# Storing the two halves of a weight unit as interleaved pairs in a two-block transformer on one core

## The chip, the cores and the metric

The kernel runs on one core of a Trainium2 chip, in one launch. The metric is the device time in microseconds from the first to the last instruction of a run; three runs of the kernel before gave 1748.44 us as their median (1747.19 to 1749.85).

## What is computed

A 256-token sequence of width 1024 goes through two layers of a first block and one layer of a second, all in float32. Cut to what matters here:

```python
for i in range(2):                                        # first block
    x = x + 0.5 * swiglu(rms_norm(x, ln_ffn1[i]), ffn1_w_gu[i], ffn1_w_down[i])   # width 2816
    h = rms_norm(x, ln_mix[i])
    x = x + (even_mixer if i == 0 else odd_mixer)(h, ...)  # latent attention + delta rule / sparse attention
    x = x + 0.5 * swiglu(rms_norm(x, ln_ffn2[i]), ffn2_w_gu[i], ffn2_w_down[i])
    x = x + sigmoid(rms_norm(x, ln_ple[i]) @ ple_w_gate[i]) * (p[i] @ ple_w_in[i])
h = rms_norm(x, norm1_g)                                  # second block
pa, pb, pg, pc = split(h @ w_in)                          # gated conv, linear recurrence, gates, rwkv
m = gate_a * y_a + gate_b * y_b + gate_c * y_c
x = x + m @ w_out
x = x + square(relu(rms_norm(x, norm2_g) @ mlp_w1)) @ mlp_w2   # width 4096
return rms_norm(x, final_g)
```

Nearly all arithmetic is in the weight products `h @ w`.

## The kernel before, in words

All weights are cut into 514 *units* of 128 partitions x 1024 float32 numbers. They come from memory in the order of use, into a ring of three slots, `raw`. A product in float32 accuracy is made out of single-pass products of rounded numbers: ScalarE copies a unit from `raw` into `w_hi` with rounding to the type fp32r (`act_split`, the activation on L456), VectorE subtracts that from `raw` and writes the remainder into `w_lo` (`dve_split`, the tensor_tensor on L464), and TensorE then multiplies low by high, high by low and high by high into one PSUM bank (`mm3`, L477; all matmuls are issued in `mm`, on L475). The activations are held in the same way as a rounded half and a remainder (`h`, `h_of_feed_forward`, `a_hi` and `a_lo`).

`w_hi` and `w_lo` are two tensors of three slots each, so that the 1024 numbers of one half lie side by side. In most products the weights are the *stationary* operand: a LDWEIGHTS reads 128 columns of one half (512 bytes of a partition, side by side), and a MATMUL then streams 256 or 512 token columns, the *moving* operand, past them. In a few products the parts are swapped, and 256 or 512 columns of a weight unit are the moving operand: the mlp's down products (`tokens_down`, L820), the value projection of the first mixer (L1390) and of the second (L2039).

The stages, in order: `ffn0`, `even`, `ffn1`, `ple0`, `ffn2`, `odd`, `ffn3`, `ple1`, `second`, `mlp`. In a gated feed-forward each of 22 rounds takes three units: two up products (`up_product`, L496: for each of 8 row tiles, w_lo against 256 columns, and w_hi against 512, which are the rounded half and the remainder of h side by side), and one down product (`down`, L837: 8 x 3 matmuls of 256 columns). A projection of the other stages (`linear`, L507) is 8 x 3 matmuls of 256 columns. `opening` and `early_units` do the same in another order at the start of a stage.

What sets the order: each engine runs its own program, written out by hand. `s_hi` and `s_lo` count split units, `s_prod` counts units whose products are done. ScalarE splits unit u when its load has landed and the products of unit u-3 are done; VectorE follows on `s_hi`; TensorE waits for `s_lo`; SyncE (SP) loads unit u+3 into `raw` once `s_lo` says that unit u has been split. The rest of ScalarE's and VectorE's work stands between the splits in their queues. POOL issues only a few transfers. Small spare tensors (`in_front_of_h`, `behind_h`, `in_front_of_a`) fix at which addresses h, raw, the weights and a begin; the edit leaves them as they are.

Of the kernel before, what the change touches and what calls it, by code (L numbers as in the profile page):

```python
# [11 lines left out]
T, P, D = 256, 128, 1024  # L12
KT = D // P
NB = T // P
UNIT = 8 * P
RING = 3
TURN = 6
D_FF, D_FF2 = 2816, 4096
FJ, FJ2 = D_FF // P, D_FF2 // P
# [267 lines left out]
def build(nc, a_x, a_p, a_w, a_par, a_con, a_gain, out, stages=STAGES):  # L287
    f32 = mybir.dt.float32
    ALU, ACT, AX = mybir.AluOpType, mybir.ActivationFunctionType, mybir.AxisListType
    MUL, ADD, SUB, MAXOP, MINOP = ALU.mult, ALU.add, ALU.subtract, ALU.max, ALU.min  # L290
    par_off, par_n = offsets(PARAMS)
    con_off, con_n = offsets(CONSTS)
    unit_base, total_units = {}, 0
# [5 lines left out]
    with ctx:  # L299
# [6 lines left out]
        def sbr(name, shape):  # L306

            return ctx.enter_context(nc.sbuf_tensor(name, shape, mybir.dt.float32r))
# [6 lines left out]
        h_hi, h_lo = h[:, :, 0, :], h[:, :, 1, :]  # L315
        sb("behind_h", [P, 88])
        raw = sb("raw", [P, RING, UNIT])
        w_hi, w_lo = sbr("w_hi", [P, RING, UNIT]), sbr("w_lo", [P, RING, UNIT])
        sb("in_front_of_a", [P, 8])
        a_hi, a_lo = sbr("a_hi", [P, 3, T]), sbr("a_lo", [P, 3, T])  # L320
        par = sb("par", [P, par_n + 8])[:, 0:par_n]
# [5 lines left out]
        ps = ctx.enter_context(nc.psum_tensor("ps", [P, 8, 512], f32))  # L327
# [6 lines left out]
        def f(ap):  # L334

            return ap.bitcast(f32)
# [44 lines left out]
        s_hi, s_lo, s_prod = sem("hi_ready"), sem("lo_ready"), sem("products_done")  # L381
# [41 lines left out]
        V, A, TE = nc.vector, nc.scalar, nc.tensor  # L423
        
        class Links:


            n = 0
# [15 lines left out]
        narrow = {unit_base["second"] + 2 + 12 * t + 7: 5 * P for t in range(KT)} if "second" in stages else {}  # L444
        if "even" in stages:
            narrow[unit_base["even"] + 25] = 2 * P
        split_next = {"act": 0, "dve": 0}

        def act_split(act, last, i=None):

            for u in range(split_next["act"], min(last + 1, total_units)):
                act.wait_ge(arrived[u % RING], loads(u, i))
                if u >= RING:
                    act.wait_ge(s_prod, nth(u - RING, i))
                n = narrow.get(u, UNIT)
                A.activation(w_hi[:, u % RING, 0:n], raw[:, u % RING, 0:n], ACT.Copy).then_inc(s_hi, 1)  # L456
                split_next["act"] = u + 1

        def dve_split(dve, last, i=None):

            for u in range(split_next["dve"], min(last + 1, total_units)):
                dve.wait_ge(s_hi, nth(u, i))
                n = narrow.get(u, UNIT)
                V.tensor_tensor(w_lo[:, u % RING, 0:n], raw[:, u % RING, 0:n], f(w_hi[:, u % RING, 0:n]), SUB)\  # L464
                    .then_inc(s_lo, 1)
                split_next["dve"] = u + 1

# [6 lines left out]
        def mm(o, lhsT, rhs, start=True, stop=True):  # L474
            return TE.matmul(o, lhsT, rhs, start=start, stop=stop, skip_group_check=True)  # L475

        def mm3(o, l_hi, l_lo, r_hi, r_lo, start=True, stop=True):  # L477

            mm(o, l_lo, r_hi, start, False)
            mm(o, l_hi, r_lo, False, False)  # L480
            return mm(o, l_hi, r_hi, False, stop)

        def wmm(o, u, k, hi, lo, start=True, stop=True):

            c_ = slice(k * P, k * P + P)
            return mm3(o, w_hi[:, u % RING, c_], w_lo[:, u % RING, c_], hi, lo, start, stop)

        def after_mixer(n):

# [6 lines left out]
        def up_product(pe, u, bank, n, i=None):  # L496

            h_ = h_of(n)

            pe.wait_ge(s_lo, nth(u, i))  # L500
            for k in range(KT):
                c_ = slice(k * P, k * P + P)
                mm(ps[:, bank, 0:T], w_lo[:, u % RING, c_], h_[:, k, 0, :], k == 0, False)
                last = mm(ps[:, bank, :], w_hi[:, u % RING, c_], h_[:, k, :, :].rearrange("p a t -> p (a t)"), False, k == KT - 1)
            last.then_inc(s_prod, 1)

        def linear(pe, u, o, i=None, norm=None, normed=None, src=None):  # L507
# [12 lines left out]
        def early_units(pe, n, tiles):  # L520

            src = h_of(n)
            for i_, (u, bank) in enumerate(tiles):
                pe.wait_ge(s_lo, nth(u))
                for k in range(KT):
                    c_ = slice(k * P, k * P + P)
                    if i_ == 0 and k % 2 == 0:
                        pe.wait_ge(s_hr, h_at[n] + k // 2 + 1)
                    mm(ps[:, bank, 0:T], w_lo[:, u % RING, c_], src[:, k, 0, :], k == 0, False)
                    mm(ps[:, bank, 0:T], w_hi[:, u % RING, c_], src[:, k, 0, :], False, False)  # L530
            for i_, (u, bank) in enumerate(tiles):
                for k in range(KT):
                    if i_ == 0 and k % 2 == 0:
                        pe.wait_ge(s_h, h_at[n] + k // 2 + 1)
                    last = mm(ps[:, bank, 0:T], w_hi[:, u % RING, k * P:k * P + P], src[:, k, 1, :], False, k == KT - 1)
                last.then_inc(s_prod, 1)


# [73 lines left out]
        def opening(pe, n, tiles):  # L612

            h_ = h_of(n)

            last_pair = KT - 2 if n and stages[n - 1] in n_ple else KT
            for ks in (range(last_pair), range(last_pair, KT)):
                for i_, (u, bank) in enumerate(tiles):
                    pe.wait_ge(s_lo, nth(u))
                    o = ps[:, bank, 0:T]  # L620
                    for k in ks:
                        c_ = slice(k * P, k * P + P)
                        if i_ == 0 and k % 2 == 0:
                            pe.wait_ge(s_hr, h_at[n] + k // 2 + 1)
                        mm(o, w_lo[:, u % RING, c_], h_[:, k, 0, :], k == 0, False)
                        mm(o, w_hi[:, u % RING, c_], h_[:, k, 0, :], False, False)
            for i_, (u, bank) in enumerate(tiles):
                o = ps[:, bank, T:2 * T]
                for k in range(KT):
                    if i_ == 0 and k % 2 == 0:  # L630
                        pe.wait_ge(s_h, h_at[n] + k // 2 + 1)
                    last = mm(o, w_hi[:, u % RING, k * P:k * P + P], h_[:, k, 1, :], False, k == KT - 1)
                last.then_inc(s_prod, 1)

        def sum_bank(n):
# [177 lines left out]
        def ffn_pe(pe, f_):  # L813
# [6 lines left out]
            def tokens_down(u, j, q, stop):  # L820

                b_, c_ = slice(q // 2 * P, q // 2 * P + P), slice(q % 2 * 512, q % 2 * 512 + 512)
                l_hi, l_lo = a_hi[:, j % f_.bufs, b_], a_lo[:, j % f_.bufs, b_]
                return mm3(ps[:, q, :], l_hi, l_lo, w_hi[:, u % RING, c_], w_lo[:, u % RING, c_], False, stop)

            def last_tokens_down():

# [220 lines left out]
        def even_mixer():  # L1048
            u0 = unit_base["even"]
# [92 lines left out]
            def pe_prog(pe):  # L1142
# [65 lines left out]
                for n in range(22):  # L1208
# [5 lines left out]
                    elif n > 1:  # L1214
                        linear(pe, u0 + n, ps[:, in_bank(n), 0:T], normed=order["even"] if n == 5 else None,
                               src=h_two if n < 5 else None)
# [169 lines left out]
                pe.wait_ge(s_lo, nth(u0 + 26))  # L1386
                for tb in range(NB):
                    for k in range(2):
                        sl, c_ = (u0 + 26) % RING, slice(k * 512, (k + 1) * 512)
                        last = mm3(ps[:, (5, 4)[tb], :], h_hi[:, 3 + k, blk(tb)], h_lo[:, 3 + k, blk(tb)],  # L1390
                                   w_hi[:, sl, c_], w_lo[:, sl, c_], k == 0, k == 1)
                last.then_inc(s_prod, 1)
                Yl(3)
                sa("qn1")
# [3 lines left out]
                for tb in range(NB):  # L1398
                    for j in range(2):
                        o = 8 * tb + 4 * j  # L1400
                        mm(ps[:, 7, o:o + 4], sq_r[:, j, blk(tb)], C("quads"), True, False)
                        for m in (2 * j, 2 * j + 1):
                            last = mm(ps[:, 7, 8 * tb + 2 * m:8 * tb + 2 * m + 2], sq_n[:, m, blk(tb)],
                                      pairs[:, 0:P:64], False, m % 2 == 1)
# [7 lines left out]
                for j in range(2):  # L1412
                    last = mm(ps[:, 6, j * T:j * T + T], heads_r[0:16, j, :], rrk[0:16, :])
# [12 lines left out]
                for g in range(4):  # L1426
                    last = mm(ps[:, 0, g * P:g * P + P], TTf[:, 0, g, :], vtok[:, 0, g, :])
# [4 lines left out]
                for g in range(4):  # L1432
                    last = mm(ps[:, 2, g * P:g * P + P], ktok[:, g, :], vn[:, g, :])
                did(last, "st0")
                for g in range(4):
                    last = mm(ps[:, 1, g * P:g * P + P], vn[:, g, :], QK[:, 0, g, :])
# [4 lines left out]
                for g in range(4):  # L1441
                    last = mm(ps[:, 0, g * P:g * P + P], kbg[:, g, blk(1)], St[:, g, :])
# [433 lines left out]
        def odd_mixer():  # L1876
            u0 = unit_base["odd"]
# [43 lines left out]
            def pe_prog(pe):  # L1921
# [108 lines left out]
                for n in (15, 16):  # L2030
                    if n == 15:
                        sa("in13")
                    u = u0 + n
                    pe.wait_ge(s_lo, nth(u))
                    for j in range(4):
                        k = 4 * (n - 15) + j
                        for tb in range(NB):
                            c_ = slice(j * T, j * T + T)
                            last = mm3(ps[:, 4 + tb, 0:T], h_hi[:, k, blk(tb)], h_lo[:, k, blk(tb)],  # L2039
                                       w_hi[:, u % RING, c_], w_lo[:, u % RING, c_], k == 0, k == 7)  # L2040
                    last.then_inc(s_prod, 1)
                    between(n)
                sa("sdq")
# [1422 lines left out]
```

## Time and profile before

| | |
|---|---|
| median of the three runs shown | 1748.44 us (1747.19 to 1749.85) |
| span of the profiled execution | 1751.1 us; the page gives it no other time |
| TensorE matmul / weight load busy | 97% / 90% |
| VectorE / ScalarE busy | 74% / 57% |
| chain that ended last | PE 83%, VectorE 8%, ScalarE 6% |
| mean granted TensorE clock | 0.982 of full speed |

A matmul row's duration is longer than the distance to the next matmul's start, since matmuls are pipelined; how fast a stream goes is read from the distances between starts. PEld rows are the weight loads, which run while an earlier matmul streams. A row that says x7 has seven instructions merged, from the first one's start to the last one's end. The line named for a wait or an operation is a line of the listing above; L475 holds every matmul that the weight products issue.

### The profile page before, as it was taken

The numbers are of one execution on the slowest core, as the hardware profiler recorded it, in microseconds if no ns is written. First come the engines' busy times: TensorE is split into PE (matmuls) and PEld (weight loads), VectorE is DVE, ScalarE is ACT, GpSimd is POOL, SyncE is SP. The second block draws the span as 40 slices with busy tenths as digits, with TensorE's granted clock in tenths as the row PEclk, the third lists the DMA queues.
The fourth block names the chain that finished last, engine by engine and source line by source line (L and its number), as shares of the span: only waits on it lengthen the run. The fifth ranks groups of instructions, "written<-read, shape, count | busy, mean of one in ns | idle before, by whom it ended". The sixth has DMA issues, their size and how long they took to land.

```text
span 1751.1 us, 37772 instructions
## 1 busy us (share of the span) xinstructions
PE 1694.5 (97%) x14502; PEld 1574.0 (90%) x14502; DVE 1290.8 (74%) x2137; ACT 995.2 (57%) x1562; POOL 3.0 (0%) x9
## 2 busy tenths in 40 slices
PE   7999999999999999999999999989999999899998
PEld 6999899889999989999988999989999998798887
DVE  6777867658777887777767777877788774567776
ACT  5544655445444664445555554668877875444444
POOL 0000000000000000000000000000000000000000
PEclk9999989899999999999999999999999999999999
DMA  6555533115555445554425655545555550055554
GB/s 230 191 188 183 165 133 109 62 31 181 192 191 188 162 166 192 180 191 157 145 82 173 192 188 188 169 157 184 178 183 191 175 163 4 23 174 179 186 187 144
DMA packets 75864, 278.24 MB, mean 159 GB/s; under 512 B 8432, under 2 KB 8688, under 8 KB 75248
## 3 DMA queue, kind: packets, MB, share of 16 engines
q1 hardware_dynamic: 75168, 273.58, 47.9%
q0 software_dynamic: 592, 3.15, 0.5%
q8 instruction: 81, 1.33, 0.3%
q14 instruction: 23, 0.19, 0.0%
HBM read 274.59 MB, written 2.10 MB: 158 GB/s over the span
## 4 chain that ended last, share of the span: by engine, by line
PE 83%; DVE 8%; ACT 6%; issue 2%; DMA 0%; DVEq 0%; SPq 0%; ACTq 0%
PE ps L475 82%; DVE w_lo L464 2%; ACT w_hi L456 2%; PE ps L2471 1%; DVE rstd L607 1%; DVE x L943 1%; DVE h L568 1%; DVE arena L911 0%; DVE arena L915 0%; ACT L2796 0%; ACT L2780 0%; DMA x<-x_t 0%; DVE arena L656 0%; DVE a_lo L931 0%; ACT arena L2133 0%
## 5 line engine op out<-in xcount | busy, mean ns | idle before, releaser
L475 PE MATMUL ps<-h,w_hi 128*128 128x256 f32 (+1 forms) x3380 | 732.4, 307 | 0.0
L464 DVE TENSOR_TENSOR w_lo<-raw,w_hi 128x1024 fp32r<-128x1024 f32 x514 | 621.4, 1215 | 86.6 <-ACT w_hi L456 67.5
L456 ACT ACTIVATE w_hi<-raw 128x1024 fp32r<-128x1024 f32 x514 | 538.6, 1050 | 223.2 <-PE ps L475 205.6
L475 PE MATMUL ps<-h,w_lo 128*128 128x256 f32 x2026 | 583.9, 289 | 22.9 <-DVE w_lo L464 15.6
L475 PEld LDWEIGHTS ps<-h,w_hi 128*128 128x128 f32 x3380 | 554.4, 193 | 26.4
L475 PEld LDWEIGHTS ps<-h,w_lo 128*128 128x128 f32 x2026 | 390.5, 193 | 30.1 <-DVE w_lo L464 14.5
L475 PE MATMUL ps<-h_of_feed_forward,w_hi 128*128 128x512 f32 (+1 forms) x1088 | 351.5, 374 | 0.0
L475 PE MATMUL ps<-h_of_feed_forward,w_lo 128*128 128x256 f32 x1000 | 278.8, 281 | 0.8 <-issue 0.6
L896 ACT ACTIVATE arena<-ps 128x256 f32<-128x256 f32 x208 | 79.1, 382 | 267.7 <-PE ps L475 267.7
L475 PEld LDWEIGHTS ps<-h_of_feed_forward,w_hi 128*128 128x128 f32 x1088 | 198.3, 188 | 36.3
L475 PE MATMUL ps<-a_hi,w_lo 128*128 128x256 f32 x776 | 218.3, 281 | 4.2 <-DVE a_lo L931 4.2
L475 PE MATMUL ps<-a_lo,w_hi 128*128 128x256 f32 x776 | 217.3, 280 | 0.0
L475 PE MATMUL ps<-a_hi,w_hi 128*128 128x256 f32 x776 | 217.0, 280 | 0.0
L911 DVE TENSOR_TENSOR arena<-ps,arena 128x256 f32<-128x256 f32 x208 | 88.3, 424 | 142.3 <-ACT arena L896 141.8
L475 PEld LDWEIGHTS ps<-h_of_feed_forward,w_lo 128*128 128x128 f32 x1000 | 188.2, 188 | 3.3 <-ACT h_of_feed_forward L560 1.2
L475 PEld LDWEIGHTS ps<-a_hi,w_lo 128*128 128x128 f32 x776 | 146.0, 188 | 6.0 <-DVE a_lo L931 5.5
L475 PEld LDWEIGHTS ps<-a_lo,w_hi 128*128 128x128 f32 x776 | 146.1, 188 | 3.2
L475 PEld LDWEIGHTS ps<-a_hi,w_hi 128*128 128x128 f32 x776 | 146.0, 188 | 0.0
L475 PE MATMUL ps<-arena 64*64 64x64 f32 (+6 forms) x2808 | 112.5, 241 | 9.3 <-issue 6.7
L475 PEld LDWEIGHTS ps<-arena 64*64 64x64 f32 (+3 forms) x2808 | 100.0, 147 | 21.3 <-issue 12.5
L915 DVE TENSOR_TENSOR arena<-arena,rstd 128x256 f32<-128x256 f32 x176 | 75.1, 427 | 6.0
L901 ACT ACTIVATE arena<-arena 128x256 f32<-128x256 f32 x120 | 50.1, 418 | 46.2 <-DVE arena L917 33.3
(354 smaller groups left out, 1447.9 us busy)
## 6 DMA issues: line engine op xcount, KB each, us to landing
raw<-weights SPq DMA_DIRECT2D x514, 512.0 KB, 3.4
con<-shape_constants SPq DMA_DIRECT2D x1, 1618.0 KB, 10.5
x<-x_t SPq DMA_DIRECT2D x1, 1024.0 KB, 5.0
stored<-x POOLq DMA_DIRECT2D x1, 1024.0 KB, 4.8
x<-stored POOLq DMA_DIRECT2D x1, 1024.0 KB, 7.9
out_t<-arena SPq DMA_DIRECT2D x4, 256.0 KB, 2.1
arena<-p_t POOLq DMA_DIRECT2D x2, 256.0 KB, 4.1
arena<-final_gain POOLq DMA_DIRECT2D x1, 512.0 KB, 4.6
```

What stands on the lines that cost most here:

```text
L456: A.activation(w_hi[:, u % RING, 0:n], raw[:, u % RING, 0:n], ACT.Copy).then_inc(s_hi, 1)
L464: V.tensor_tensor(w_lo[:, u % RING, 0:n], raw[:, u % RING, 0:n], f(w_hi[:, u % RING, 0:n]), SUB)\
L475: return TE.matmul(o, lhsT, rhs, start=start, stop=stop, skip_group_check=True)
L568: last = V.scalar_tensor_tensor(h_[:, k, 1, :], x[:, k, :], G(NORM_OF[stages[n]], k), f(h_[:, k, 0, :]), MUL, SUB)
L607: V.reciprocal(rstd[:, :], rstd[:, :]).then_inc(s_vc, vc.step())
L896: A.activation(rest[:, half, j % f_.bufs, :], ps[:, f_.bank(j) + half, T:2 * T], ACT.Copy).then_inc(s_rest, 1)
L901: A.activation(sg[:, j % f_.bufs, :], tg[:, j % f_.bufs, :], ACT.Silu if f_.gated else ACT.Square).then_inc(s_nl, 1)
L911: V.tensor_tensor((t_, u_)[half], ps[:, f_.bank(j) + half, 0:T], rest[:, half, j % f_.bufs, :], ADD)\
L915: V.tensor_tensor((t_, u_)[half], (t_, u_)[half], rstd[:, :], MUL).then_inc((s_scl, s_fac)[half], 1)
L943: V.scalar_tensor_tensor(x[:, pair_of(b), :], ps[:, b, :].rearrange("p (a t) -> p a t", a=2), 0.5, x[:, pair_of(b), :], MUL, ADD).then_inc ...
L2471: last = TE.transpose(ps[:, bk, s * P:s * P + P], two_heads(src, c, s), ident)
```

## The change

`w_hi` and `w_lo` become one tensor `w` of three slots of 2048 numbers. In a slot, element n of the unit has its rounded half at place 2n and its remainder at 2n+1. ScalarE writes the halves at a step of 8 bytes, VectorE reads them and writes the remainders at that step, and every LDWEIGHTS of a weight half reads 128 numbers at that step, over 1024 bytes instead of 512. Units in the set `planar`, those that are the moving operand, keep the old form inside a slot: 1024 halves, then 1024 remainders. They are 1 unit of `even`, 2 of `odd` and the 32 down units of `mlp`, 35 of 514. No instruction is added, removed or moved, and the size in memory is the same.

```diff
-        w_hi, w_lo = sbr("w_hi", [P, RING, UNIT]), sbr("w_lo", [P, RING, UNIT])
+        w_ = sbr("w", [P, RING, 2 * UNIT])
...
+        planar = set()
+        if "even" in stages:
+            planar.add(unit_base["even"] + 26)
+        if "odd" in stages:
+            planar |= {unit_base["odd"] + 15, unit_base["odd"] + 16}
+        if "mlp" in stages:
+            planar |= set(range(unit_base["mlp"] + 2, unit_base["mlp"] + 2 * FJ2 - 4, 2))
+            planar |= {unit_base["mlp"] + 2 * FJ2 - n for n in (3, 2, 1)}
+
+        def parts_of(u, cols):
+
+            slot = w_[:, u % RING, :]
+            if u in planar:
+                return slot[:, 0:UNIT][:, cols], slot[:, UNIT:2 * UNIT][:, cols]
+            pairs_ = slot.rearrange("p (n two) -> p n two", two=2)
+            return pairs_[:, cols, 0], pairs_[:, cols, 1]
...
-                A.activation(w_hi[:, u % RING, 0:n], raw[:, u % RING, 0:n], ACT.Copy).then_inc(s_hi, 1)
+                A.activation(parts_of(u, slice(0, n))[0], raw[:, u % RING, 0:n], ACT.Copy).then_inc(s_hi, 1)
...
-                V.tensor_tensor(w_lo[:, u % RING, 0:n], raw[:, u % RING, 0:n], f(w_hi[:, u % RING, 0:n]), SUB)\
+                hi, lo = parts_of(u, slice(0, n))
+                V.tensor_tensor(lo, raw[:, u % RING, 0:n], f(hi), SUB)\
                     .then_inc(s_lo, 1)
...
-            return mm3(o, w_hi[:, u % RING, c_], w_lo[:, u % RING, c_], hi, lo, start, stop)
+            return mm3(o, *parts_of(u, c_), hi, lo, start, stop)
...
-                mm(ps[:, bank, 0:T], w_lo[:, u % RING, c_], h_[:, k, 0, :], k == 0, False)
-                last = mm(ps[:, bank, :], w_hi[:, u % RING, c_], h_[:, k, :, :].rearrange("p a t -> p (a t)"), False, k == KT - 1)
+                mm(ps[:, bank, 0:T], parts_of(u, c_)[1], h_[:, k, 0, :], k == 0, False)
+                last = mm(ps[:, bank, :], parts_of(u, c_)[0], h_[:, k, :, :].rearrange("p a t -> p (a t)"), False, k == KT - 1)
...
-                return mm3(ps[:, q, :], l_hi, l_lo, w_hi[:, u % RING, c_], w_lo[:, u % RING, c_], False, stop)
+                return mm3(ps[:, q, :], l_hi, l_lo, *parts_of(u, c_), False, stop)
```

The other matmuls of weight units (`early_units`, `opening`, the two value projections) change in the same way.

## Rows read from the trace of the kernel before

**Rows 1.** The page: busy time by engine, and the chain that ended last.
```profile
PE 1694.5 (97%) x14502; PEld 1574.0 (90%) x14502; DVE 1290.8 (74%) x2137; ACT 995.2 (57%) x1562; POOL 3.0 (0%) x9
...
PE 83%; DVE 8%; ACT 6%; issue 2%; DMA 0%; DVEq 0%; SPq 0%; ACTq 0%
```

**Rows 2.** Windows: a feed-forward, a stretch of second, mlp; columns as headed.
```profile
core 0: us, PE busy (x) PEld busy (x) DVE busy (x) ACT busy (x) POOL busy (x), PEclk, DMA share, GB/s
27.00:195.00 168.00, 167.86 (x1126) 154.62 (x1127) 130.53 (x205) 83.81 (x123) 0.00 (x0) 1.00 0.58 187
1220.00:1240.00 20.00, 20.00 (x167) 19.75 (x167) 16.24 (x32) 18.27 (x32) 0.00 (x0) 1.00 0.49 167
1572.00:1736.00 164.00, 164.00 (x825) 138.25 (x824) 114.14 (x175) 81.25 (x117) 0.00 (x0) 1.00 0.56 179
```

**Rows 3.** Timeline, PE, first feed-forward: start us, length us, line, operands.
```profile
109.87 0.39 PE L475 MATMUL ps<-h,w_hi 128*128 128x512 f32 x1
110.10 0.28 PE L475 MATMUL ps<-h,w_lo 128*128 128x256 f32 x1
...
110.56 0.39 PE L475 MATMUL ps<-h,w_hi 128*128 128x512 f32 x1
110.79 0.28 PE L475 MATMUL ps<-a_hi,w_lo 128*128 128x256 f32 x1
...
112.89 0.28 PE L475 MATMUL ps<-a_hi,w_lo 128*128 128x256 f32 x1
```

**Rows 4.** Timeline, PE, a projection of second.
```profile
1370.74 0.28 PE L475 MATMUL ps<-h,w_lo 128*128 128x256 f32 x1
1370.86 0.40 PE L475 MATMUL ps<-h,w_hi 128*128 128x256 f32 x2
...
1373.23 0.28 PE L475 MATMUL ps<-h,w_lo 128*128 128x256 f32 x1
```

**Rows 5.** Timeline, PE, a projection of ple0.
```profile
611.92 0.28 PE L475 MATMUL ps<-h,w_lo 128*128 128x256 f32 x1
612.04 0.40 PE L475 MATMUL ps<-h,w_hi 128*128 128x256 f32 x2
...
612.64 0.28 PE L475 MATMUL ps<-h,w_lo 128*128 128x256 f32 x1
```

**Rows 6.** Groups by shape, PE: count | busy us, mean ns | idle us before.
```profile
L475 PE MATMUL ps<-h,w_lo 128*128 128x256 f32 x2026 | 583.9, 289 | 22.9 <-DVE w_lo L464 15.6 <-DVE h L652 4.8 <-ACT h L560 1.9
L475 PE MATMUL ps<-h,w_hi 128*128 128x256 f32 x2708 | 497.3, 286 | 0.0
L475 PE MATMUL ps<-h_of_feed_forward,w_lo 128*128 128x256 f32 x1000 | 278.8, 281 | 0.8 <-issue 0.6
L475 PE MATMUL ps<-h,w_hi 128*128 128x512 f32 x672 | 235.1, 392 | 0.0
L475 PE MATMUL ps<-a_hi,w_lo 128*128 128x256 f32 x776 | 218.3, 281 | 4.2 <-DVE a_lo L931 4.2
L475 PE MATMUL ps<-h_of_feed_forward,w_hi 128*128 128x256 f32 x176 | 31.6, 281 | 0.0
L475 PE MATMUL ps<-con,arena 128*128 128x1 f32 x124 | 15.0, 253 | 1.1 <-DVE arena L602 0.8 <-ACT arena L1543 0.3
```

**Rows 7.** Timeline, PE: matmuls of one moving column, each with its weight load.
```profile
277.10 0.92 PE L475 MATMUL ps<-con,arena 128*128 128x1 f32 x7
```

**Rows 8.** Groups by shape, weight loads of 128 and of 64 columns.
```profile
L475 PEld LDWEIGHTS ps<-h_of_feed_forward,w_hi 128*128 128x128 f32 x1088 | 198.3, 188 | 36.3
L475 PEld LDWEIGHTS ps<-con,arena 128*64 128x64 f32 x64 | 3.3, 135 | 1.5 <-DVE arena L3023 0.6
```

**Rows 9.** Groups by shape: L3156 at a step of 8 bytes, L3210 side by side, the splits.
```profile
L3156 DVE TENSOR_TENSOR x<-x,arena 128x512 f32<-128x512 f32 x2 | 1.4, 694 | 0.1
L3210 DVE TENSOR_TENSOR arena<-arena 128x512 f32<-128x512 f32 x4 | 2.8, 692 | 0.1
L464 DVE TENSOR_TENSOR w_lo<-raw,w_hi 128x1024 fp32r<-128x1024 f32 x505 | 614.4, 1222 | 86.6 <-ACT w_hi L456 67.5
L456 ACT ACTIVATE w_hi<-raw 128x1024 fp32r<-128x1024 f32 x505 | 532.2, 1056 | 214.0 <-PE ps L475 196.4 <-DMA raw<-weights 11.3 <-DVE arena L2949 2.7
L456 ACT ACTIVATE w_hi<-raw 128x640 fp32r<-128x640 f32 x8 | 5.9, 738 | 9.2 <-PE ps L475 9.2
```

More of the change, by code:

```diff
@@ L528, in early_units @@
                         pe.wait_ge(s_hr, h_at[n] + k // 2 + 1)
-                    mm(ps[:, bank, 0:T], w_lo[:, u % RING, c_], src[:, k, 0, :], k == 0, False)
-                    mm(ps[:, bank, 0:T], w_hi[:, u % RING, c_], src[:, k, 0, :], False, False)
+                    mm(ps[:, bank, 0:T], parts_of(u, c_)[1], src[:, k, 0, :], k == 0, False)
+                    mm(ps[:, bank, 0:T], parts_of(u, c_)[0], src[:, k, 0, :], False, False)
             for i_, (u, bank) in enumerate(tiles):
@@ L534, in early_units @@
                         pe.wait_ge(s_h, h_at[n] + k // 2 + 1)
-                    last = mm(ps[:, bank, 0:T], w_hi[:, u % RING, k * P:k * P + P], src[:, k, 1, :], False, k == KT - 1)
+                    last = mm(ps[:, bank, 0:T], parts_of(u, slice(k * P, k * P + P))[0], src[:, k, 1, :], False, k == KT - 1)
                 last.then_inc(s_prod, 1)
@@ L624, in opening @@
                             pe.wait_ge(s_hr, h_at[n] + k // 2 + 1)
-                        mm(o, w_lo[:, u % RING, c_], h_[:, k, 0, :], k == 0, False)
-                        mm(o, w_hi[:, u % RING, c_], h_[:, k, 0, :], False, False)
+                        mm(o, parts_of(u, c_)[1], h_[:, k, 0, :], k == 0, False)
+                        mm(o, parts_of(u, c_)[0], h_[:, k, 0, :], False, False)
             for i_, (u, bank) in enumerate(tiles):
@@ L631, in opening @@
                         pe.wait_ge(s_h, h_at[n] + k // 2 + 1)
-                    last = mm(o, w_hi[:, u % RING, k * P:k * P + P], h_[:, k, 1, :], False, k == KT - 1)
+                    last = mm(o, parts_of(u, slice(k * P, k * P + P))[0], h_[:, k, 1, :], False, k == KT - 1)
                 last.then_inc(s_prod, 1)
@@ L1388, in pe_prog @@
                     for k in range(2):
-                        sl, c_ = (u0 + 26) % RING, slice(k * 512, (k + 1) * 512)
+                        c_ = slice(k * 512, (k + 1) * 512)
                         last = mm3(ps[:, (5, 4)[tb], :], h_hi[:, 3 + k, blk(tb)], h_lo[:, 3 + k, blk(tb)],
-                                   w_hi[:, sl, c_], w_lo[:, sl, c_], k == 0, k == 1)
+                                   *parts_of(u0 + 26, c_), k == 0, k == 1)
                 last.then_inc(s_prod, 1)
@@ L2039, in pe_prog @@
                             last = mm3(ps[:, 4 + tb, 0:T], h_hi[:, k, blk(tb)], h_lo[:, k, blk(tb)],
[L2040 removed]
+                                       *parts_of(u, c_), k == 0, k == 7)
                     last.then_inc(s_prod, 1)
```

## The prediction

> **What bounds the kernel now.** I read the page first: the matmul row is busy for 97% of the span, the weight-load row for 90%, and 83% of the chain that ended last is PE [rows 1]. Busy matmuls prove little, so the windows by stage come next. In a feed-forward, in `second` and in `mlp` PE is covered from end to end at a granted clock of 1.00 (the 2.4 GHz level), while VectorE has 37 us of 168 free and ScalarE 84 [rows 2]. So in these stages the end is set by how close matmuls follow each other, and the timeline gives that. In the feed-forward 18 down matmuls of 256 columns take 112.89 - 110.79 = 2.10 us, 116.7 ns each; two up pairs (256 and 512 columns) take 110.56 - 109.87 = 0.69 us, 345 ns a pair, so that 228 ns are left for the 512 columns [rows 3]. In a projection of `second` 21 matmuls of 256 columns take 1373.23 - 1370.74 = 2.49 us, 118.6 ns each [rows 4]; in one of `ple0` six take 0.72 us, 120.0 ns [rows 5]. The same shape thus runs at three paces, all at full clock.
>
> What stands beside such a matmul is the load of the next 128 weights. Seven matmuls of a single moving column take 0.92 us, of which the last one's own length is 0.253 us, so one follows the other after (0.92 - 0.25) / 6 = 111 ns [rows 6, 7]; with nothing to stream, that is the pace of the load. A load of 128 columns is recorded with 188 ns and one of 64 with 135 [rows 8]: 0.83 ns a column. So matmul and load are nearly tied, 117 to 120 ns against 111. With 512 columns the load ends within the first half, and the second half costs at most 228 - 116.7 = 111 ns: an upper estimate of what 256 columns cost when no load runs beside them. Between 5 and 9 ns of each 256-column matmul are thus more than either stream needs alone.
>
> **The change part by part.** No instruction comes, goes or moves, so no queue is passed and no wait added; three kinds of operand change their step.
>
> *The splits on VectorE.* It reads the halves and writes the remainders at 8 bytes. The trace has such an operation: L3156 reads and writes x at every second number, and 512 elements take 694 ns against 692 side by side [rows 9]. Cost: 0.
>
> *The splits on ScalarE.* It writes at 8 bytes; no row shows that engine doing so. Lower bound 0, since even the form side by side is no faster than 0.83 ns an element ((1056 - 738) / 384 [rows 9]) and a step gives no reason for gain; upper bound one more 0.83 ns an element, 0.85 us a split. I take 0, from the nearest row, VectorE's. In a feed-forward ScalarE's 84 free microseconds would cover 60 splits of +0.85 us (51 us); in `second` it is busy 18.27 of 20 us [rows 2], and the cover is thin (a rival below).
>
> *The planar units.* They keep their order inside a slot; 0.
>
> *The weight loads.* Matmuls of 256 columns on stationary units: 2026 + 2708 + 1000 + 176 and three times 776 (the low-by-high down form and its two companions), 8238 in all [rows 6]. Of these, 2708 x 1.5 = 4062 belong to projections, which run at 118.6; the other 4176 run at about 116.7. After the change a load covers 1024 bytes at 0.83 ns a column, 8 bytes each, and the moving operand covers 1024 bytes in nearly the same time; before, the load went through 512. The two streams therefore advance side by side instead of one overtaking the other. Where they share something in the memory, that either frees them from each other or keeps them in step at the bad place. Outer bound of a gain: all 256-column matmuls down to 111 ns, 4062 x 7.6 + 4176 x 5.7 = 55 us. Outer bound of a loss: a load that takes twice its time per column, 111 + 128 x 0.83 = 217 ns, then sets the pace: 4062 x 98 + 4176 x 100 = +817 us. The first fits a stream that meets no other, the second a load that can fetch only one number where it now fetches two; no row shows a stationary read at a step. VectorE's row speaks against the second. I take the nearest row to the first that is actually sustained in this kernel, 116.7 ns: the projections fall from 118.6 to 116.7, 4062 x 1.9 = 7.7 us, all of it on PE's own path, because PE is covered in those windows. The 512-column matmuls hide the load either way: 0.
>
> Sum: -7.7 us. The span of the profiled execution is 1751.1 us and the median of the runs 1748.4, 0.15% less; the difference carries over, so 1748.4 - 7.7 = 1741 us. Next late would be ScalarE in `second`, at 18.27 of then 19.7 us.
>
> The Trainium skill speaks against this gain: "TensorE: Matmul & The Clock Gate", section "Step-by-step: what each phase is for", says that weights and moving data come through two independent read ports, so that a load takes no bandwidth from a running matmul. By it the sum is 0, and the same-time case below holds. The trace agrees only in part, since one shape runs at 116.7, 118.6 and 120.0 ns at one clock [rows 3 to 5].
>
> **The rivals.**
> *Nothing moves.* The 5 to 9 ns over 111 are the two streams' own handshake, or the moving stream's own fetch, and the load keeps its pace. For it: 512 columns cost 228, close to twice 116.7, so most of the excess goes with moving columns and not with loads. Against: three paces of one shape. 1748 us.
>
> *Slower: the streams collide all along.* A load that touches twice the addresses, in step with the moving operand, meets it more often. All 256-column matmuls then run at the worst pace seen, 120.0 ns [rows 5]: 4062 x 1.4 + 4176 x 3.3 = +19.5 us, 1768 us. It decides as soon as the common pace is above 117.6, the weighted mean of now. For it: the load has only 6 to 9 ns of room. Against: the nearest step-of-8 row cost nothing.
>
> *Slower: ScalarE becomes the bound in `second`.* With 24 x 118.6 ns = 2.85 us a unit, seven units lie in 20 us, so ScalarE has 1.73 / 7 = 0.25 us a unit free. A split longer than 1056 + 250 ns decides; at +0.85 us each of about 98 units costs 0.60 us, +59 us, 1807 us.
>
> *A load twice as long:* up to 1748 + 817 = 2565 us.
>
> *Much faster:* the streams part completely, down to 1748 - 55 = 1693 us. For it only the 111 ns of the second half.
>
> *That the change doesn't do what it says* I exclude: the operands' steps are in the text of the kernel.
>
> **How the numbers follow.** The forecast, 1741 us, gets 0.36; much faster 0.08; nothing moves 0.27; collision 0.17; ScalarE 0.08; the long load 0.04. Below 0.2% (3.5 us, about what a measurement of this kernel can tell from none) counts as same. So faster 0.44, same 0.27, slower 0.29. The range 1715 to 1775 holds the forecast, nothing moves, most of the collision case (0.15) and the near part of much faster (0.03), 0.81 together; the likeliest case's own range is 1735 to 1745, projections at 115.5 to 118 ns.
>
> **What would show it.** In the changed profile: the down matmuls' distance near 116.7 and the projections' falling to it (forecast), staying at 118.6 (nothing moves), or both at 120 and above (collision); LDWEIGHTS still at 188 ns, and single-column matmuls, whose operands don't change, still at 111; L456's successor at 1.05 us and L464's at 1.22. The prediction is wrong if the loads lengthen beyond the matmuls, if ScalarE's split passes 1.3 us, or if the 512-column pairs move from 345 ns, since I gave them nothing.

## The result, and the profile after

The changed kernel takes 1776.05 us (median of four runs, 1772.54 to 1776.7), the kernel before 1747.82 beside it (1747.1 to 1749.85): a ratio of 1.0157, interval 1.0142 to 1.0171. It is slower by 28 us, where 7.7 us less were forecast, and it lies 1 us above the range. The profiled execution has a span of 1774.3 us against 1751.1, a difference of 23.2.

The page of the changed kernel, in its first part and its chain:

```profile
span 1774.3 us, 37772 instructions
...
PE 1717.4 (97%) x14502; PEld 1604.7 (90%) x14502; DVE 1292.8 (73%) x2137; ACT 1033.7 (58%) x1562; POOL 3.0 (0%) x9
...
PE 87%; DVE 7%; ACT 4%; issue 2%; DMA 0%; SPq 0%; DVEq 0%; ACTq 0%
```

Against [rows 1], the matmul row grew by 22.9 us, about as much as the span, and the weight-load row by 30.7; VectorE stayed, ScalarE grew by 38.5, and the chain has more PE and less of both. So the time is on PE's own path. The windows of the changed kernel, a feed-forward and a stretch of `second`, columns as in [rows 2]:

```profile
27.00:195.00 168.00, 168.00 (x1108) 156.31 (x1108) 127.89 (x200) 86.25 (x120) 0.00 (x0) 1.00 0.57 184
1220.00:1240.00 20.00, 20.00 (x168) 19.65 (x167) 16.32 (x28) 15.61 (x22) 0.00 (x0) 1.00 0.53 174
```

The clock is the same 1.00 and PE is covered as before, but 1108 matmuls fit in the feed-forward's 168 us instead of 1126. Nobody waits longer; the matmuls follow each other more slowly. The timeline of the changed kernel's first feed-forward, PE:

```profile
106.15 5.79 PE L492 MATMUL ps<-h,w 128*128 128x256 f32 x32
111.78 0.28 PE L492 MATMUL ps<-a_hi,w 128*128 128x256 f32 x1
111.89 0.28 PE L492 MATMUL ps<-a_lo,w 128*128 128x256 f32 x1
...
114.55 0.28 PE L492 MATMUL ps<-a_hi,w 128*128 128x256 f32 x1
```

The first row holds 16 up pairs (a row that merges instructions carries the shape of the first of them): (111.78 - 106.15) / 16 = 352 ns a pair. The 23 down matmuls behind it take (114.55 - 111.78) / 23 = 120.4 ns each. In `second`, 52 matmuls on h (same view):

```profile
1368.83 6.44 PE L492 MATMUL ps<-h,w 128*128 128x256 f32 x52
```

That is (6.44 - 0.28) / 51 = 120.8 ns. The following means are of the distances between the starts of neighbouring matmuls (for a pair, from one pair's start to the next one's), over the whole of each trace; distances with a pause or a stretch of half clock in them (above 140 ns for 256 columns) are left out:

| | before | after | difference x count |
|---|---|---|---|
| projections on h, 256 columns | 118.07 ns | 120.67 | 4062 x 2.60 = +10.6 us |
| down, 256 columns | 116.90 | 120.66 | 2328 x 3.76 = +8.8 us |
| up pairs, 256 + 512 columns | 346.99 | 351.32 | 1584 x 4.33 = +6.9 us |
| mlp's planar down, 512 columns | 233.4 | 233.4 | 0 |

The sum, some 26 us, is 3 us more than the difference of the spans and lies inside the interval of the ratio (24.8 to 29.9 us). The products whose weight loads step by 8 bytes became slower, the planar ones did not. The groups by shape of the changed kernel (count | busy us, mean ns | idle before):

```profile
L492 PEld LDWEIGHTS ps<-h_of_feed_forward,w 128*128 128x128 f32 x2088 | 321.6, 195 | 35.7 <-ACT h_of_feed_forward L577 1.1 <-issue 0.7
L492 PEld LDWEIGHTS ps<-w,a_hi 128*128 128x128 f32 x256 | 48.1, 188 | 11.5
L481 DVE TENSOR_TENSOR w<-raw,w 128x1024 fp32r<-128x1024 f32 x505 | 616.4, 1223 | 116.6 <-ACT w L472 103.1
L472 ACT ACTIVATE w<-raw 128x1024 fp32r<-128x1024 f32 x505 | 577.7, 1146 | 209.6 <-PE ps L492 192.5 <-DMA raw<-weights 11.0 <-DVE arena L2966 2.7
```

A load at a step is recorded 7 ns longer than the 188 of [rows 8]; one that reads a_hi side by side (second row) is not longer. VectorE's split kept its time [rows 9], ScalarE's grew from 1056 to 1146 ns. Two suspects are left: the reading of the stationary operand at a step, and the writing at a step, which lengthened ScalarE's split.

### The profile page after: what moved, and what is told of

Its sections match the earlier page's. It is cut to its first block, busy times and chain, and to the rows that moved or that the text cites. A ratio compares the mean times of both kernels' runs of the same rounds, so it can differ in the third digit from the quotient of the medians.

```text
span 1774.3 us, 37772 instructions
## 1 busy us (share of the span) xinstructions
PE 1717.4 (97%) x14502; PEld 1604.7 (90%) x14502; DVE 1292.8 (73%) x2137; ACT 1033.7 (58%) x1562; POOL 3.0 (0%) x9
## 4 chain that ended last, share of the span: by engine, by line
PE 87%; DVE 7%; ACT 4%; issue 2%; DMA 0%; SPq 0%; DVEq 0%; ACTq 0%
PE ps L492 86%; DVE w L481 2%; ACT w L472 1%; PE ps L2488 1%; DVE rstd L624 1%; DVE h L585 1%; DVE arena L928 0%; DVE x L960 0%; DMA x<-x_t 0%; DVE arena L673 0%; ACT h L577 0%; DVE arena L932 0%; ACT arena L2150 0%; ACT arena L599 0%; DVE a_lo L948 0%
## 5 line engine op out<-in xcount | busy, mean ns | idle before, releaser
L492 PE MATMUL ps<-h,w 128*128 128x256 f32 (+1 forms) x5406 | 766.9, 303 | 22.7 <-DVE w L481 15.7
L492 PEld LDWEIGHTS ps<-h,w 128*128 128x128 f32 x5406 | 721.8, 200 | 53.2 <-DVE w L481 14.5
L472 ACT ACTIVATE w<-raw 128x1024 fp32r<-128x1024 f32 x514 | 584.6, 1140 | 218.6 <-PE ps L492 201.5
L481 DVE TENSOR_TENSOR w<-raw,w 128x1024 fp32r<-128x1024 f32 x514 | 623.4, 1215 | 116.6 <-ACT w L472 103.1
L492 PE MATMUL ps<-h_of_feed_forward,w 128*128 128x256 f32 (+1 forms) x2088 | 366.5, 331 | 0.7 <-issue 0.6
L492 PEld LDWEIGHTS ps<-h_of_feed_forward,w 128*128 128x128 f32 x2088 | 321.6, 195 | 35.7 <-ACT h_of_feed_forward L577 1.1
L492 PE MATMUL ps<-a_hi,w 128*128 128x256 f32 x1552 | 296.7, 284 | 4.2 <-DVE a_lo L948 4.2
L492 PEld LDWEIGHTS ps<-a_hi,w 128*128 128x128 f32 x1552 | 253.6, 197 | 5.7 <-DVE a_lo L948 5.5
L492 PE MATMUL ps<-a_lo,w 128*128 128x256 f32 x776 | 220.2, 284 | 0.0
L492 PEld LDWEIGHTS ps<-a_lo,w 128*128 128x128 f32 x776 | 152.6, 197 | 3.1
```

What stands on the lines that cost most here:

```text
L472: A.activation(parts_of(u, slice(0, n))[0], raw[:, u % RING, 0:n], ACT.Copy).then_inc(s_hi, 1)
L481: V.tensor_tensor(lo, raw[:, u % RING, 0:n], f(hi), SUB)\
```

## The experiments

**1. Pairs written, but read side by side.** The change alters writing and reading; this undoes the reading, the next the writing.

```diff
-        def parts_of(u, cols):
+        def parts_of(u, cols, read=True):          # both splits call it with False
...
-            if u in planar:
+            if u in planar or read:
```

> The changed kernel, in which ScalarE and VectorE still write and read pairs at a step of 8 bytes, but every weight load reads 128 numbers side by side out of the slot (so the weights multiplied are a mixture of halves and remainders: this part of the computation is changed). Theory A (the stationary read at a step costs the time): loads return to 188 ns, down matmuls follow each other at 116.7 ns and not 120.8, the 512-column ones at 229.5 and not 233, and the time is that of the kernel before, 1748 us, within 4 us; ScalarE's split stays at 1140 ns. Theory B (the writes at a step disturb TensorE's reads): the time stays at 1776 us, matmuls at 120.8. Theory C (ScalarE's longer split, 1140 against 1050 ns, holds the stages back): also 1776 us, with matmuls closer together and gaps between units.

Measured: 1749.51 us, ratio 1.0005 (0.999 to 1.002). Its timeline in the first feed-forward, PE, and its groups by shape:

```profile
104.47 5.71 PE L492 MATMUL ps<-h,w 128*128 128x256 f32 x32
110.02 0.28 PE L492 MATMUL ps<-a_hi,w 128*128 128x256 f32 x1
...
112.70 0.28 PE L492 MATMUL ps<-a_hi,w 128*128 128x256 f32 x1
```
```profile
L492 PEld LDWEIGHTS ps<-a_lo,w 128*128 128x128 f32 x776 | 145.9, 188 | 3.3
...
L472 ACT ACTIVATE w<-raw 128x1024 fp32r<-128x1024 f32 x505 | 574.6, 1140 | 199.1 <-PE ps L492 182.8 <-DMA raw<-weights 10.5 <-DVE arena L2966 2.7
```

A pair is back at (110.02 - 104.47) / 16 = 347 ns, a down matmul at (112.70 - 110.02) / 23 = 116.5, a load at 188, while ScalarE's split is as long as in the changed kernel. The longer split alone costs nothing that shows in the ratio (more on this under 2); the slow matmuls are gone with the stepped reading.

**2. Written side by side, read as pairs.** As above with the condition turned round:

```diff
+            if u in planar or not read:
```

> The changed kernel, in which ScalarE and VectorE write halves and remainders side by side, 1024 numbers each, as before, but every load of a stationary weight half reads 128 numbers at a step of 8 bytes out of the slot (the weights multiplied are thus the wrong ones of the slot: this part of the computation is changed). Theory A (stationary read): 1776 us within 4 us, loads 196 ns, down matmuls 120.8 ns, while ScalarE's split is back at 1050 ns. Theories B and C (the splits' step): 1748 us, matmuls 116.7 ns.

Measured: 1770.89 us, ratio 1.0117 (1.0092 to 1.0141). Its timeline in the first feed-forward, PE, and its split on ScalarE:

```profile
106.71 5.79 PE L492 MATMUL ps<-h,w 128*128 128x256 f32 x32
112.33 0.28 PE L492 MATMUL ps<-a_hi,w 128*128 128x256 f32 x1
...
115.11 0.28 PE L492 MATMUL ps<-a_hi,w 128*128 128x256 f32 x1
```
```profile
L472 ACT ACTIVATE w<-raw 128x1024 fp32r<-128x1024 f32 x505 | 532.3, 1056 | 226.7 <-PE ps L492 208.7 <-DMA raw<-weights 11.3 <-DVE arena L2966 2.8
```

A pair takes (112.33 - 106.71) / 16 = 351 ns and a down matmul (115.11 - 112.33) / 23 = 120.9; over the whole trace the projections run at 120.65. All three are as in the changed kernel, with ScalarE at its old 1056. Reading at a step is the cause of most of the loss: 1.17 of 1.57% by the ratios, 20 of 27 us. The two intervals just miss each other, and the rest is not in the paces of the weight products, which are the same in both traces. Runs at one granted clock can be compared more closely: at 0.985 the changed kernel took 1774.3 us and experiment 2 1770.9 (means of two runs each), and at 0.986 experiment 1 took 1749.3 (five runs) and the kernel before beside it 1747.1 (three). So the stepped writes may cost some 2 to 3.5 us by themselves, which these few runs suggest and don't show.

**3. Loads at several steps, measured by themselves.** Behind the last product of the kernel before stand groups of 32 matmuls whose results nobody reads; the step of the load, the moving columns and the start change from group to group (wf is w_hi and hf is h, each as one row of numbers):

```diff
+        for _ in range(32):                         # one group: 256 columns, a load at 8 bytes
+            TE.matmul(ps[:, 7, 0:256], wf[:, 0:256:2], hf[:, 0:256], start=True, stop=True, ...)
```

> The kernel before, with 37 groups of 32 matmuls behind its last product on TensorE, whose results nobody reads: stationary operand from the weight halves at steps of 0 to 8 numbers, 64, 256 or 512 moving columns, and at steps 1 and 2 eleven different starts of the stationary operand. Theory A1 (the load at a step is slower by itself, and sets the pace at 256 columns): with 64 moving columns, where only the load counts, one matmul follows the other after 111 ns at step 1, about 120 at step 2, more at steps 4 and 8; with 256 columns the larger of that and 117; with 512 columns 230 at every step up to 4. Theory A2 (load and moving stream meet in the memory): with 64 columns 111 ns at steps 1 and 2, with 256 columns 117 and 121, with 512 columns 230 and 233, at step 0 less than at step 1, and at step 2 the distance depends on where the stationary operand starts relative to the moving one, by 3 ns or more from start to start, more so than at step 1.

Its timeline, PE, one row a group; steps in numbers of 4 bytes: 1, 2, 3, 4, 8 with 64 moving columns, then 2, 3, 4, 8, 0 with 256 columns, last one whose moving operand steps by 2:

```profile
1741.29 3.75 PE L3329 MATMUL ps<-h,w_hi 128*128 128x64 f32 x32
1744.86 7.01 PE L3331 MATMUL ps<-h,w_hi 128*128 128x64 f32 x32
1751.68 7.01 PE L3333 MATMUL ps<-h,w_hi 128*128 128x64 f32 x32
1758.51 7.64 PE L3335 MATMUL ps<-h,w_hi 128*128 128x64 f32 x32
1765.96 7.79 PE L3337 MATMUL ps<-h,w_hi 128*128 128x64 f32 x32
...
1779.81 4.03 PE L3341 MATMUL ps<-h,w_hi 128*128 128x256 f32 x32
1783.68 5.72 PE L3343 MATMUL ps<-h,w_hi 128*128 128x256 f32 x32
1789.23 7.63 PE L3345 MATMUL ps<-h,w_hi 128*128 128x256 f32 x32
1796.70 7.84 PE L3347 MATMUL ps<-h,w_hi 128*128 128x256 f32 x32
1804.39 3.90 PE L3349 MATMUL ps<-h,w_hi 128*128 128x256 f32 x32
...
1922.05 7.56 PE L3403 MATMUL ps<-h,w_hi 128*128 128x256 f32 x32
```

The distance from one group's start to the next one's, over 32, gives the pace: 213 ns for 64 columns at steps 2 and 3 and 233 at step 4, beside 111.6 at step 1. That doubling between steps 1 and 2 was not the load's: behind the short matmuls the granted clock fell. Two windows of this run show it, columns as in [rows 2]:

```profile
1759.00:1765.00 6.00, 6.00 (x27) 6.00 (x28) 0.00 (x0) 0.00 (x0) 0.00 (x0) 0.50 0.00 0
...
1790.00:1796.00 6.00, 6.00 (x27) 6.00 (x27) 0.00 (x0) 0.00 (x0) 0.00 (x0) 1.00 0.01 3
```

The first is step 4 with 64 columns, at 0.50 (1.2 GHz), the second step 4 with 256 columns, at 1.00 (2.4 GHz). Both run at about 233 ns. With 256 columns and full clock the paces are 120.7 (step 2), 173.5 (3), 233.4 (4), 240.0 (8) and 116.7 (0). From step 4 on little more is lost (step 8 costs 3% more), which fits numbers fetched four at a time, in lines of 16 bytes: at step 2 a load of 128 numbers touches 64 lines, at step 3 96, at step 4 all 128. 233.4 / 128 = 1.823 ns a line, and 96 lines at that price are 175. The moving operand obeys it too: 256 columns side by side are 64 lines and take 116.7 ns (step 0, with almost nothing to load), and at a step of two they are 128 lines and take 230. Beside 512 columns this step of the load cost nothing from this start: 233.9 ns at steps 1 and 2, where theory A2 expected 3 ns more at step 2. With 256 columns eleven starts of the weights gave 116.6 to 120.1 ns side by side, and 120.0 to 120.9 at a step of two: the stepped load's pace hardly depends on where it starts.

The Trainium skill, "Advanced Engine Details and Errata", section "SBUF Cachelines", has lines of 16 bytes and says that two hits on a line are needed to absorb the latency. The measured paces have their knee there, 120.7 ns at two hits against 173.5 at four thirds. By that rule the second hit would make the load free; here two hits cost the 4 ns between 116.7 and 120.7, which are this case, and the measurement decides.

**4. The kernel before with its weights 128 bytes later.** If starts matter, a shift alone should move the projections, without any pairs.

```diff
+        sb("in_front_of_w", [P, 32])
```

> The kernel before with 32 spare numbers between raw and the weights, so that weights, a and the arena begin 128 bytes later relative to h and in the same place relative to each other. Theory L (a 16-byte line of memory costs about 1.8 ns on either stream, whatever the starts): the matmuls on h stay at 118.0 ns, and the time at 1748 us. Theory S (the start of the load relative to the moving operand matters while both walk at different speeds; the bench gave 116.6 to 117.8 ns at starts 32, 96, 160 and 224 numbers on, and 118.8 mostly at 0, 64, 128 and 192): matmuls of 256 columns on h fall from 118.0 to about 117, those on a and on the other h stay, 4700 x 1.0 = 4.7 us less, 1743 us.

Measured: 1743.77 us, ratio 0.9982 (0.997 to 0.9993). Projections fall from 118.07 to 116.94 ns, 4062 x 1.13 = 4.6 us, against a gain of 3.1 us by the ratio (1.2 to 5.2); down stays at 116.8.

**5. The changed kernel with the same shift.** The collision theory, that the pairs only happen to start badly against the moving operand, expects a mending here.

> The changed kernel with the same 32 spare numbers in front of the weights. Theory C (load and moving stream walk in step, and at this start they meet at the bad place all along): the matmuls on h move by 2 ns or more, down if the new place is good, and the time by 8 us or more from 1776. Theory L (the load at a step of 8 bytes has as many 16-byte lines as 256 moving columns, 64, and is paced by them, wherever it starts): 120.3 ns and 1776 us as without, within 3 us.

Measured: 1775.7 us, ratio 1.0162 (1.0143 to 1.0181); projections at 120.64 ns, where they took 120.67 without the shift. This start does not rescue the pairs, and neither did the eleven starts of experiment 3, so for the 256-column products the theory falls. In the up products the start does count: their pairs on h went from 351.4 to 353.4 ns (more under 11).

**6. A second bench at full clock.** Groups of 24, each behind a stretch of 512-column matmuls that brings the clock back up; and pairs of 256 and 512 columns with either load at a step.

> The kernel before with a second set of matmul groups behind it; each group of few columns follows 40 matmuls of 512 columns, so that it meets the full clock. Theory L: with 64 or 128 moving columns, where the load alone sets the pace, 111 ns at a step of 1 number, 117 to 120 at 2 (64 lines), 173 at 3 (96 lines), 233 at 4 (128 lines). Theory A2 (the load at 2 is as fast as at 1 by itself and only meets the stream): 111 at steps 1 and 2. Alternating matmuls of 256 and 512 columns: by L the pair takes 345 ns when the 256-column matmul's own load is at a step (it runs beside 512 columns), and 3 ns more when the 512-column one's is (it runs beside 256). Step 1, eight starts of the moving operand in 32-byte steps: by theory S a spread of 2 ns or more between them, by L less than 1.

Its timeline, PE: 64 columns at steps 1, 2 and 4, and 128 columns at step 2:

```profile
1752.34 2.76 PE L3331 MATMUL ps<-h,w_hi 128*128 128x64 f32 x24
...
1764.37 2.92 PE L3335 MATMUL ps<-h,w_hi 128*128 128x64 f32 x24
...
1794.23 5.59 PE L3343 MATMUL ps<-h,w_hi 128*128 128x64 f32 x24
...
1823.41 2.98 PE L3351 MATMUL ps<-h,w_hi 128*128 128x128 f32 x24
```

With hardly anything to stream, the load alone takes 111.7 ns at step 1, 117.8 at step 2, some 173 at step 3 (read from the group's part at full clock) and 233.3 at step 4; with 128 columns 111.6 and 120.0 at steps 1 and 2. So step 1 is bound by columns, and at step 2 the lines have just overtaken them: 64 x 1.823 = 116.7 ns against 111.7. Beside 128 columns, half of what the kernel streams, the stepped load already takes 120.0: 2 ns come from the longer stream beside it, and by what is not shown. Eight starts of the moving operand gave 117.3 to 119.9 ns with the load side by side, and four gave 120.0 to 120.9 with it at a step. A pair takes 346.9 ns with no load at a step, 351.0 with both, and 346.9 or 346.7 with only one of them. With one fixed address for every load, a single step was harmless here; the kernel walks through addresses.

**7 and 8. Only the up products' low, or only their high loads at a step.** Theory L: the load that runs beside the 512 columns (the low one, used next) is hidden. Theory M: it meets the stream in the memory wherever it runs.

```diff
+        def parts_of(u, cols, read=False):          # everything written and read side by side, except
...
-                mm(ps[:, bank, 0:T], parts_of(u, c_)[1], h_[:, k, 0, :], k == 0, False)
+                mm(ps[:, bank, 0:T], parts_of(u, c_, True)[1], h_[:, k, 0, :], k == 0, False)
```

> The second experiment's kernel, in which only the loads of the remainder in the up products read at a step of 8 bytes (wrong weights there); these loads run beside a 512-column matmul. Theory L (a load of 120 ns is hidden behind 230): 512-column matmuls stay at 229.6 ns, 256-column ones at 117.5, time 1748 us. Theory M (a load at a step slows the moving stream beside it): 512-column matmuls 233 ns, 1584 x 3.5 = 5.5 us more, 1754 us.

> The counterpart of the fourth-listed run with low loads: only the loads of the rounded half in the up products read at a step of 8 bytes (wrong weights there); these run beside a 256-column matmul. Theory L: the 256-column matmuls before them go from 117.5 to 118.7 to 120 ns, the 512-column ones stay at 229.6, 1584 x 1.2 to 2.5 = 2 to 4 us more than 1748. Theory M as well (a load at a step slows the stream that it runs beside, by more than its own length): 256-column matmuls above 121 ns. If the extra 3.7 ns of the 512-column matmuls belonged to reading their own weights at a step, they would show 233 here.

Measured: low 1753.36 us, ratio 1.0044 (1.003 to 1.0057); high 1750.56, ratio 1.0016 (1.0004 to 1.0029). The timelines in the first feed-forward, PE, first with the low loads at a step, then two stretches with the high ones:

```profile
104.84 5.78 PE L492 MATMUL ps<-h,w 128*128 128x256 f32 x32
110.46 0.28 PE L492 MATMUL ps<-a_hi,w 128*128 128x256 f32 x1
```
```profile
105.69 5.73 PE L492 MATMUL ps<-h,w 128*128 128x256 f32 x32
111.25 0.28 PE L492 MATMUL ps<-a_hi,w 128*128 128x256 f32 x1
...
114.05 5.77 PE L492 MATMUL ps<-h,w 128*128 128x256 f32 x32
119.66 0.28 PE L492 MATMUL ps<-a_hi,w 128*128 128x256 f32 x1
```

The 16 pairs take 351 ns each in the first, 347.5 and 350.6 in the others. Over the whole traces pairs take 351.0 ns with the low loads at a step and 349.3 with the high ones: 1584 x 4.0 = 6.4 us and 1584 x 2.3 = 3.6 us, which is 0.37% and 0.21%. L falls: a load at a step can cost time even where 512 columns cover it twice. (How a pair's time divides between its two matmuls isn't readable, since a matmul's recorded start can lie before the end of its own load: in experiment 10 the two starts are mostly 117 ns apart, though loads come 175 ns apart there where they set the pace.)

**9. The kernel before with weights and arena 128 bytes later.** The arena holds the feed-forwards' h.

```diff
+        sb("in_front_of_w", [P, 32])
...
+        sb("in_front_of_arena", [P, 32])
```

> The kernel before with 32 spare numbers in front of the weights, as in the fastest run so far (0.9982 of before), and 32 more in front of the arena, in which the other rounded activations lie. Theory S (the start of the stationary relative to the moving operand counts): the matmuls on the arena's h, 117.5 and 229.8 ns, go where those on h went, 117.1 and 228.4, about 2 us less than 1744. Without it: 1744 us.

Measured: 1743.34 us, ratio 0.9967 (0.9956 to 0.9979), faster than both kernels. Projections are at 116.82 ns (4062 x 1.25 = 5.1 us of the 5.8 that the ratio gives), in the trace of `second`, PE, 15 of them in 1.76 us:

```profile
1363.51 0.28 PE L477 MATMUL ps<-h,w_lo 128*128 128x256 f32 x1
...
1365.27 0.28 PE L477 MATMUL ps<-h,w_lo 128*128 128x256 f32 x1
```

The 256-column half of the pairs on the arena's h was a miss: expected 117.1, recorded 118.2. Its other half came as expected, 228.6 for 228.4, and the whole pair moved only from 347.2 to 346.8.

**10. Loads at three numbers.** If lines set the pace, a load of 96 lines must take 173 ns in the kernel itself.

```diff
-            pairs_ = slot.rearrange("p (n two) -> p n two", two=2)
-            return pairs_[:, cols, 0], pairs_[:, cols, 1]
+            first, n = cols.start, cols.stop - cols.start
+            return tuple(slot[:, first + half:first + half + 3 * n - 2:3] for half in (0, 1))
```

> The second experiment's kernel (splits side by side) with the loads of stationary halves at a step of 12 bytes instead of 8, 96 lines of 16 bytes instead of 64 (wrong weights). Theory L: 1.8 ns a line, so 173 ns for each 256-column matmul, 8238 x (173 - 117.6) = 456 us more than before, 2204 us, while 512-column matmuls hide a load of 173 and stay under 240 ns. A pace of the load by columns alone (0.83 ns each) with a small fixed extra for any step: about 1776 us as with 8 bytes.

Measured: 2202.36 us, ratio 1.2604 (1.2575 to 1.2633), 2 us from the expected time. Its groups by shape, and its timeline in a feed-forward, PE:

```profile
L492 PEld LDWEIGHTS ps<-a_lo,w 128*128 128x128 f32 x776 | 204.8, 264 | 0.0
```
```profile
128.80 6.79 PE L492 MATMUL ps<-h,w 128*128 128x256 f32 x32
135.43 0.28 PE L492 MATMUL ps<-a_hi,w 128*128 128x256 f32 x1
135.55 0.34 PE L492 MATMUL ps<-a_lo,w 128*128 128x256 f32 x1
...
139.22 0.34 PE L492 MATMUL ps<-a_lo,w 128*128 128x256 f32 x1
```

21 down matmuls take 139.22 - 135.55 = 3.67 us, 174.8 ns each; a load is recorded with 264 ns, 76 more than the 188 of [rows 8] (and 175 - 111 = 64). A pair takes (135.43 - 128.80) / 16 = 414 ns. The expectation of under 240 ns for its 512 columns can't be read, for the reason given under 7 and 8; the pair takes 67 ns more than before in any case. That the total comes within 2 us is in part luck: by these paces (57 ns more for some 6650 matmuls, 67 for 1584 pairs) the span would have grown by 485 us, and it grew by 449. The lines' price stands by the 174.8 ns, not by the total.

**11. Pairs that walk through the addresses.** As in 6, but each pair takes the next columns, as the kernel does.

> The kernel before with a third set of groups behind it: 32 pairs each of a 256-column matmul (low) and a 512-column one (high), walking over the eight row tiles of h as the up product does, with the low loads at a step of 8 bytes from eight starts, only the high ones, both, and neither. If the extra of the 512-column matmuls is a meeting of the load beside them with the moving stream, a pair takes 346 ns at some starts and 350 or more at others with only the low loads at a step; if it is the load's length alone, every start gives 346.

Its timeline, PE: the first and the last pair without a step, then the first and the last with only the low load at a step, 31 pairs each:

```profile
1747.94 0.28 PE L3332 MATMUL ps<-h,w_hi 128*128 128x256 f32 x1
...
1758.69 0.28 PE L3332 MATMUL ps<-h,w_hi 128*128 128x256 f32 x1
1759.04 0.28 PE L3336 MATMUL ps<-h,w_hi 128*128 128x256 f32 x1
...
1769.94 0.28 PE L3336 MATMUL ps<-h,w_hi 128*128 128x256 f32 x1
```

Without a step 10.75 / 31 = 346.8 ns, with it 10.90 / 31 = 351.6. By the start of the low load (0, 1, 8, 16, 24, 32, 40, 48 numbers) the pair takes 351.8, 351.8, 350.9, 350.0, 349.9, 351.7, 352.0 and 347.0 ns; with only the high load at a step it takes 347.3 and 346.7, with both 351.0 and 353.3. Without any step it takes 350.9 from start 8 and 346.6 from start 32. So a load and a stream do meet, by address, even side by side; with the low load at a step seven of the eight starts that were tried are bad ones. Which addresses meet, and in what, stays open: the starts tried give no rule, and in the kernel (8) the high loads cost 2 ns, which this bench doesn't show.

## Why the prediction was wrong

*The place* was right: PE's own path, set by the distances between matmuls at full clock, with no wait that grew (PE waited 15.6 us for the splits' remainders before and 15.7 after).

*The step that failed* is the weight loads: "After the change a load covers 1024 bytes at 0.83 ns a column, 8 bytes each". The 0.83 ns is the pace of a load that finds four numbers in each line. I took the columns as what a load costs and never asked what the bytes under them cost, though the moving stream's 116.7 ns for 1024 bytes stood in [rows 3]. Runs 3 and 6 give the missing term: 1.8 ns a line, so that 64 lines take the load alone to 117.8 ns instead of 111.7, over the 116.7 of the matmul that had hidden it; beside a stream of 128 columns it takes 120.0, beside 256 the two run at 120.0 to 120.9. A margin of 5 ns became a bound. Of the 4 ns from 116.7 to 120.7 the lines by themselves explain 1; the rest comes when a stream runs beside the load, and by what stays open. The gain that I hung on it (projections falling to 116.7) came out as +2.6 ns, and the down products, which I left as they were, took 3.8 more.

*The 512-column matmuls at 0* failed as well: a pair went from 347 to 351 ns, +6.9 us, a quarter of the sum. That 512 columns "hide the load either way" holds for the load's length (117.8 of 233 ns), but not for its meeting with the stream (7 and 11).

*The base* was mis-sized: I read 118.6 ns off one projection; the mean over all is 118.07, so that even the gain as imagined would have been 4062 x 1.4 = 5.6 us.

*The rivals.* The collision case had the sign and nearly the size, 120.0 ns for all 256-column matmuls and 1768 us (measured 120.7 for projections and down), and its words "the load has only 6 to 9 ns of room" were the ones to weigh. Of the pairs it counted the 256-column half alone. Its mechanism is half right: the load touches twice the lines, and beside a stream it takes 2 to 3 ns more than alone, but it also became longer by itself (6), and for the 256-column products other starts don't mend it (3 and 5). The outer bound of a doubled load (111 + 106 = 217 ns) was no phantom: at two numbers more of step, experiment 3 has 233. "Nothing moves" is excluded by the interval.

*The Trainium skill's rule* of two independent read ports ("TensorE: Matmul & The Clock Gate", section "Step-by-step: what each phase is for"), weighed there, does not hold for these pairs: they take 346.6 or 350.9 ns with the same loads and streams, by the address of the loads alone (11). It put the forecast's gain rightly in doubt, but by it the change would cost nothing.

*VectorE's split at 0* was right (1222 to 1223 ns). *ScalarE's at 0* was wrong by 90 ns of the 850 that bounded it; it had cover for the most part, in `second` too (experiment 1 has the long split and a ratio of 1.0005; perhaps 2 to 3.5 us, see 2), and the point of 1306 ns from which it would decide was not reached. *The planar units at 0* were right: 233.4 ns before and after, loads at 188.

*Open:* how much of the last 0.4% between experiment 2 and the changed kernel the stepped writes cost, why a stepped load takes 2 to 3 ns more beside a stream than alone, and the addresses at which loads and streams meet.

## What to carry to other kernels

Before giving a hidden load a step, count what it touches and not only what it delivers: here a load of 128 weights cost the larger of its columns (111.7 ns) and its 16-byte lines (1.8 ns each), at 64 lines 2 to 3 ns more beside a stream, and it stays hidden only as long as that is below the stream it stands beside. Where two streams are tied within a few nanoseconds thousands of times over, a term of 3 ns is some 25 us (here 26 us over 7974 matmuls and pairs), so measure the disputed operand by itself, in a loop behind the kernel and at the clock that the kernel has. Moving a tensor by 128 bytes costs an unused strip of memory, and here two such strips were worth 5.8 us, most of the 7.7 that the change was meant to bring.

## What was not expected of the hardware

- The price of a line doesn't follow TensorE's clock: a load at step 4 took 232.8 ns at a granted 0.50 and 233.4 at 1.00. What is paced by columns does: 111.7 ns at step 1 with full clock, and 213.3 at half clock, there at steps 2 and 3 alike, since 64 or 96 lines fit under it.
- 256 moving columns of four bytes took 116.7 ns with almost nothing to load, 230.5 or 229.7 at a step of two: the moving operand pays by lines as well.
- ScalarE took 1146 ns instead of 1056 to write 1024 numbers 8 bytes apart (1140 in experiment 1), VectorE's split took no longer than before.
- With loads side by side, one and the same matmul of 256 columns ran at 116.6 to 120.1 ns, by the start of its weights; two shifts of 128 bytes took 0.33% off the kernel before.
